# Two products of 512 and 256 columns in place of three of 256: the feed-forward of a four-layer transformer stack

## The reference

```python
# first kind, D_FF = 2816, conv over 3 tokens
def conv_glu_ffn(h, w_gate, w_up, conv_w, w_down):
    gate = causal_dwconv(h @ w_gate, conv_w)
    return (jax.nn.gelu(gate, approximate=True) * (h @ w_up)) @ w_down
# second kind, D_FF_2 = 4096, and a gate over all of x behind it
    m = jnp.square(jax.nn.relu(h @ w_up)) @ w_down
    x = x + rmsnorm(m, g_post_mlp)
    x = x + jax.nn.sigmoid(x @ w_ple_gate) * (p_i @ w_ple_proj)
```

## Time and profile before

| | |
|---|---|
| median of 3 runs | 1665.17 us (1662.94 to 1671.31) |
| the profiled execution | 1663.27 us |
| its span, first to last instruction | 1661.5 us |
| PE / DVE / ACT busy | 95% / 66% / 47% |
| mean granted TensorE clock | 0.974 of 2.4 GHz |

### The profile page before, as it was taken

One profiled execution on the slowest core, in us unless ns is written; L12 is line 12 of the kernel. 1 busy time (PEld: TensorE's weight loads), 2 busy tenths in 40 slices (PEclk: granted clock), 3 DMA queues, 4 the chain that ended last, 5 costly groups with the idle time before them and its releaser, 6 DMA issues.

```text
span 1661.5 us, 29327 instructions
## 1 busy us (share of the span) xinstructions
PE 1570.3 (95%) x11996; PEld 1402.5 (84%) x11996; DVE 1096.8 (66%) x1593; ACT 777.1 (47%) x1167; POOL 0.2 (0%) x4
## 2 busy tenths in 40 slices
PE   7998988999999989799999899899999989899998
PEld 7986568998898856799989788799889888799887
DVE  3765667776477576677754887666455698766545
ACT  4534254444445333644444365755345346755434
POOL 0000000000000000000000000000000000000000
PEclk9999898999999979899999899999999989999999
DMA  7521033655642201465554333455555333355553
GB/s 252 164 71 52 1 98 122 203 179 200 193 142 68 78 27 35 135 199 180 201 192 126 101 107 120 137 188 196 193 187 141 121 102 102 127 178 192 201 178 102
DMA packets 186310, 232.23 MB, mean 140 GB/s; under 512 B 22560, under 2 KB 161600, under 8 KB 186048
## 3 DMA queue, kind: packets, MB, share of 16 engines
q1 hardware_dynamic: 186176, 230.34, 43.0%
HBM read 229.28 MB, written 1.05 MB: 139 GB/s over the span
## 4 chain that ended last, share of the span: by engine, by line
PE 81%; DVE 7%; ACT 4%; DVEq 2%; issue 2%; DMA 2%; ACTq 1%; SPq 0%
PE banks L434 80%; DVE all_ring_rounded L2759 1%; ACT all_ring_rounded L2577 1%; DVE all_rest L2928 1%; DVE all_work L2863 1%; DMA all_ring<-in_w_in 1%; DMA all_ring<-in_w_ple_gate 1%; DVEq L2862 1%; PE banks L2242 1%; DVE all_work L2825 1%; PE banks L928 0%; DVE all_work L2821 0%; DVE all_work L2847 0%; ACT all_work L345 0%; DVEq L2823 0%
## 5 line engine op out<-in xcount | busy, mean ns | idle before, releaser
L434 PE MATMUL banks<-all_mix_rounded,all_ring_rounded 128*128 128x256 f32 (+2 forms) x3584 | 661.0, 285 | 15.6 <-DVEq L430 12.1
L434 PEld LDWEIGHTS banks<-all_mix_rounded,all_ring_rounded 128*128 128x128 f32 (+2 forms) x3584 | 561.6, 191 | 24.5 <-DVEq L430 13.7
L434 PE MATMUL banks<-all_work_rounded,all_ring_rounded 128*128 128x256 f32 x1792 | 508.1, 284 | 0.0
L434 PE MATMUL banks<-all_ring_rounded,all_work_rounded 128*128 128x512 f32 (+1 forms) x1856 | 463.0, 377 | 0.7 <-DVE all_ring_rounded L2759 0.7
L434 PEld LDWEIGHTS banks<-all_ring_rounded,all_work_rounded 128*128 128x128 f32 x1856 | 349.1, 189 | 66.3 <-issue 2.3
L434 PEld LDWEIGHTS banks<-all_work_rounded,all_ring_rounded 128*128 128x128 f32 x1792 | 343.2, 192 | 1.3 <-issue 1.0
L2759 DVE TENSOR_TENSOR all_ring_rounded<-all_ring,all_ring_rounded 128x2048 fp32r<-128x2048 f32 x104 | 237.6, 2291 | 137.5 <-ACT all_ring_rounded L2577 134.5
L1610 DVE TENSOR_TENSOR all_ring_rounded<-all_ring,all_ring_rounded 128x2048 fp32r<-128x2048 f32 (+2 forms) x96 | 214.1, 2233 | 87.5 <-ACT all_ring_rounded L1367 84.6
L2577 ACT ACTIVATE all_ring_rounded<-all_ring 128x2048 fp32r<-128x2048 f32 x104 | 198.2, 1910 | 152.5 <-DMA all_ring<-in_w_mlp_down 87.4
L1367 ACT ACTIVATE all_ring_rounded<-all_ring 128x2048 fp32r<-128x2048 f32 (+2 forms) x96 | 177.9, 1860 | 93.0 <-DMA all_ring<-in_ffn_w_down 42.3
L434 PE MATMUL banks<-all_work 64*64 64x64 f32 (+10 forms) x2084 | 169.5, 275 | 22.5 <-ACT all_work L2581 5.5
(11 more groups left out here) (263 smaller groups left out, 1232.7 us busy)
## 6 DMA issues: line engine op xcount, KB each, us to landing
all_ring<-in_w_in SPq DMA_DIRECT2D x48, 1024.0 KB, 5.4
all_ring<-in_w_mlp_up SPq DMA_DIRECT2D x32, 1024.0 KB, 5.4
all_ring<-in_w_mlp_down SPq DMA_DIRECT2D x32, 1024.0 KB, 4.9
all_ring<-in_ffn_w_gate SPq DMA_DIRECT2D x22, 1024.0 KB, 5.4
all_ring<-in_ffn_w_up SPq DMA_DIRECT2D x22, 1024.0 KB, 5.5
all_ring<-in_ffn_w_down SPq DMA_DIRECT2D x22, 1024.0 KB, 5.0
all_ring<-in_w_out SPq DMA_DIRECT2D x16, 512.0 KB, 4.2
all_ring<-in_w_out SPq DMA_DIRECT2D x8, 1024.0 KB, 5.0
```

What stands on the lines that cost most here:

```text
L434: ins = self.nc.tensor.matmul(out, lhsT, rhs, start=start, stop=stop)
```

## The change

In gate, up and block 2's up, a k tile takes two products. The weights' high part now streams against both parts of h at once, 512 columns, into a whole bank: high by high in its first half, high by low in its second. The weights' low part streams against h's high part, 256 columns, into the first half. What the PE no longer adds up is added by others: ACT copies the second half out, and DVE adds the first half to the copy. For this, gate and up get a bank each. In block 1, the convolution's first step (a product with one weight per partition) goes from DVE to ACT, the rounding of the product too, and the low part is taken one step later. ACT rounds the next panel in the middle of its step. In block 2 the relu is merged into DVE's square. `w_ple_gate`'s panels are cut in four k tiles by 512 columns. The two areas of h's parts become one tensor.

```diff
+    def mm_wide(self, out, w, k):
+
+        h = self.hi_and_lo[:, :, k, :]
+        if k < KT - 1:
+            self.mm(shaped(out, 2, T), w[0], h, k == 0, False)
+        last = self.mm(out[:, 0:T], w[1], h[:, 0, :], False, False)
+        if k == KT - 1:
+            last = self.mm(shaped(out, 2, T), w[0], h, False, True)
+        return last
...
@@ rows_by
-            for k in range(KT):
-                last = self.mm3(banks[q // 2][:, (q % 2) * 256:(q % 2) * 256 + 256], [a[:, k, t * P:(t + 1) * P] for a in lhs],
-                                [a[:, k, :] for a in w], k == 0, k == KT - 1)
+            for k in range(4):
+                at = 4 * (q % 2) + k
+                last = self.mm3(banks[q // 2], [a[:, at, t * P:(t + 1) * P] for a in lhs], [a[:, k, :] for a in w], at == 0, at == KT - 1)
...
@@ block 1, PE
-            c, b = (j % 2) * P, psum.bank(f"ff{j}")
+            c, name = (j % 2) * P, f"{('gate', 'up')[half]}_{j}"
+            b = psum.claim(pe, name)
             for k in range(KT):
-                last = mm3(b[:, half * T:(half + 1) * T], [a[:, k, c:c + P] for a in w], [a[:, k, :] for a in h], k == 0, k == KT - 1)
+                last = kit.mm_wide(b, [a[:, k, c:c + P] for a in w], k)
+            last.then_inc(psum.full_of(name), 1)
...
@@ block 1, ACT
-        for j in range(FT):
-            q = j // 2 + 1
-            name = f"{('gate', 'up')[j % 2]}{q}" if q < FT // 2 else f"down{j - FT + 2}"
-            round_weights(name)
-            act.wait_ge(*psum.filled(f"ff{j}"))
-            if j >= 2:
-                act.wait_ge(*due("ff_conv", j - 1))
-            A_(gpad[:, j % 2, 2:2 + T], psum.bank(f"ff{j}")[:, 0:T], ACT.Copy).then_inc(S["ff_gate"], 1)
-            act.wait_ge(*due("ff_conv", j + 1))
-            A_(gcv[:, j % 2, 2, :], gcv[:, j % 2, 1, :], ACT.Gelu_apprx_tanh).then_inc(S["ff_gelu"], 1)
+        for j in range(FT + 1):
+            if j < FT:
+                if not j:
+                    round_weights(panel_at(0))
+                act.wait_ge(*psum.filled(f"gate_{j}"))
+                A_(gpad[:, j % 2, 2:2 + T], psum.bank(f"gate_{j}")[:, T:2 * T], ACT.Copy).then_inc(S["ff_gate"], 1)
+                act.wait_ge(*psum.filled(f"up_{j}"))
+                A_(gl[:, j, :], psum.bank(f"up_{j}")[:, T:2 * T], ACT.Copy).then_inc(S["ff_up"], 1)
+                act.wait_ge(*due("ff_added", j + 1))
+                A_(gcv[:, j % 2, 0, :], gpad[:, j % 2, 2:2 + T], ACT.Copy, scale=fw[:, j, 2:3]).then_inc(S["ff_scaled"], 1)
+                if j < FT - 1:
+                    round_weights(panel_at(j + 1))
+            if j:
+                act.wait_ge(*due("ff_prod", j))
+                A_(rounded(gh[:, j - 1, :]), gcv[:, (j - 1) % 2, 2, :], ACT.Copy).then_inc(S["g_hi"], 1)
+            if j < FT:
+                act.wait_ge(*due("ff_conv", j + 1))
+                A_(gcv[:, j % 2, 2, :], gcv[:, j % 2, 1, :], ACT.Gelu_apprx_tanh).then_inc(S["ff_gelu"], 1)
...
@@ block 1, DVE (its former loop and finish(j) go)
+        def add_first_half(out, name):
+            return V.tensor_tensor(out, psum.bank(name)[:, 0:T], out, ALU.add)
+
+        def low_part(j):
+            dve.wait_ge(*due("g_hi", j + 1))
+            V.tensor_tensor(rounded(gl[:, j, :]), gcv[:, j % 2, 2, :], as_float32(rounded(gh[:, j, :])), ALU.subtract)
+            dve.drain().then_inc(S["gT"], 1)
...
+        for j in range(FT + 1):
+            if j < FT:
+                subtract_rounded(panel_at(j))
+                if j >= 2:
+                    low_part(j - 2)
+                dve.wait_ge(*due("ff_gate", j + 1))
+                add_first_half(gpad[:, j % 2, 2:2 + T], f"gate_{j}").then_inc(*psum.freed(f"gate_{j}"))
+                dve.drain().then_inc(S["ff_added"], 1)
+                dve.wait_ge(*due("ff_up", j + 1))
+                add_first_half(gl[:, j, :], f"up_{j}").then_inc(*psum.freed(f"up_{j}"))
             if j:
...
+                dve.wait_ge(*due("ff_gelu", j))
+                dve.drain()
+                V.tensor_tensor(gcv[:, (j - 1) % 2, 2, :], gcv[:, (j - 1) % 2, 2, :], gl[:, j - 1, :], ALU.mult).then_inc(S["ff_prod"], 1)
+            if j < FT:
+                dve.wait_ge(*due("ff_scaled", j + 1))
...
@@ block 2, panels
-    late += [(f"2{layer}.ple{i}", wgate[layer, :, :, 256 * i:256 * i + 256], KT, 0, 256) for i in range(4)]
+    late += [(f"2{layer}.ple{2 * half + n}", wgate[layer, :, 4 * n:4 * n + 4, 512 * half:512 * half + 512], 4, 0, 512)
+             for half in range(2) for n in range(2)]
...
@@ block 2, ACT
-                act.wait_ge(*psum.filled(f"ff{c}"))
-                A_(gh[:, 2 * c:2 * c + 2, :], shaped(psum.bank(f"ff{c}"), 2, T), ACT.Relu).then_inc(*psum.freed(f"ff{c}"))
-                act.drain().then_inc(S["ff_relu"], 1)
+                for half in range(2):
+                    act.wait_ge(*psum.filled(f"ff{c}{half}"))
+                    A_(gh[:, 2 * c + half, :], psum.bank(f"ff{c}{half}")[:, T:2 * T], ACT.Copy).then_inc(S["ff_half"], 1)
...
@@ block 2, DVE
-                V.tensor_tensor(gl[:, 2 * c:2 * c + 2, :], gh[:, 2 * c:2 * c + 2, :], gh[:, 2 * c:2 * c + 2, :],
-                                ALU.mult).then_inc(S["ff_squared"], 1)
+                for half in range(2):
+                    part = gh[:, 2 * c + half, :]
+                    dve.wait_ge(*due("ff_half", 2 * c + half + 1))
+                    V.tensor_tensor(part, psum.bank(f"ff{c}{half}")[:, 0:T], part, ALU.add).then_inc(*psum.freed(f"ff{c}{half}"))
+                dve.drain()
+                V.scalar_tensor_tensor(gl[:, 2 * c:2 * c + 2, :], gh[:, 2 * c:2 * c + 2, :], 0.0, gh[:, 2 * c:2 * c + 2, :],
+                                       ALU.max, ALU.mult).then_inc(S["ff_squared"], 1)
```

More of the change, by code:

```diff
@@ L313, in __init__ @@
         self.nc = nc
+        self.hi_and_lo = shaped(rounded(columns(0, 2 * KT * T)), 2, KT, T)
         self.x, self.columns, self.rounded, self.hT, self.mixT = x, columns, rounded, hT, mixT
@@ L640 @@
     1, "b_exp": 1, "erow": 1, "hid": 1, "decays": 1, "nt": 1, "act": 2, "lb_max": 1, "lb_exp": 1, "ff_conv": 22, "ff_gate": 22, "ff_gelu": 22,
-    "kr_done": 1, "dve": 70, "log_f": 2, "lf_tok": 2, "e_ready": 16, "kq": 16, "masked": 14, "last_scores": 2, "vf": 14, "weighed": 16, "level_U": 6,
+    "kr_done": 1, "dve": 48, "log_f": 2, "lf_tok": 2, "e_ready": 16, "kq": 16, "masked": 14, "last_scores": 2, "vf": 14, "weighed": 16, "level_U": 6,
+    "ff_scaled": 22, "ff_prod": 22, "g_hi": 22, "ff_up": 22, "ff_added": 22,
 }
@@ L760, in panels1, with panel_at @@
     return panels[:FIRST + 1] + with_parts(panels[FIRST + 1:] + late)
+def panel_at(j):
+    q = j // 2 + 1
+    return f"{('gate', 'up')[j % 2]}{q}" if q < FT // 2 else f"down{j - FT + 2}"
 def block1(nc, ctx, kit, banks, ring_all, A):
@@ L1344, in tensor @@
         for j in range(FT):
-            psum.claim(pe, f"ff{j}")
             for half in range(2):
-                last = gate_up(j, half)
-            last.then_inc(psum.full_of(f"ff{j}"), 1)
+                gate_up(j, half)
         def wait_product(n):
@@ L2011, in vector @@
         dve.drain()
-        for j in range(FT):
-            q = j // 2 + 1
-            name = f"{('gate', 'up')[j % 2]}{q}" if q < FT // 2 else f"down{j - FT + 2}"
-            subtract_rounded(name)
-            dve.wait_ge(*due("ff_gate", j + 1))
-            step(V.tensor_scalar(gcv[:, j % 2, 0, :], gpad[:, j % 2, 2:2 + T], fw[:, j, 2:3], None, ALU.mult))
-            step(V.scalar_tensor_tensor(gcv[:, j % 2, 1, :], gpad[:, j % 2, 1:1 + T], fw[:, j, 1:2], gcv[:, j % 2, 0, :], ALU.mult, ALU.add))
-            V.scalar_tensor_tensor(gcv[:, j % 2, 1, :], gpad[:, j % 2, 0:T], fw[:, j, 0:1], gcv[:, j % 2, 1, :], ALU.mult, ALU.add).then_inc(S["ff_conv"], 1)
-            if j:
-                finish(j - 1)
-        finish(FT - 1)
+        for j in range(FT + 1):
[8 more added lines that the diff above has]
+                add_first_half(gl[:, j, :], f"up_{j}").then_inc(*psum.freed(f"up_{j}"))
+            if j:
+                dve.wait_ge(*due("ff_gelu", j))
[3 more added lines that the diff above has]
+                dve.wait_ge(*due("ff_scaled", j + 1))
+                step(V.scalar_tensor_tensor(gcv[:, j % 2, 1, :], gpad[:, j % 2, 1:1 + T], fw[:, j, 1:2], gcv[:, j % 2, 0, :], ALU.mult, ALU.add))
+                V.scalar_tensor_tensor(gcv[:, j % 2, 1, :], gpad[:, j % 2, 0:T], fw[:, j, 0:1], gcv[:, j % 2, 1, :], ALU.mult, ALU.add).then_inc(S["ff_conv"], 1)
+        low_part(FT - 2)
+        low_part(FT - 1)
         for i in range(2, FT // 2):
@@ L2528, in up @@
             w = kit.split_panel(pe, ring, f"up{c}")
-            b = psum.bank(f"ff{c}")
+            b = psum.claim(pe, f"ff{c}{half}")
             for k in range(KT):
-                last = mm3(b[:, half * T:(half + 1) * T], [a[:, k, half * P:(half + 1) * P] for a in w], [a[:, k, :] for a in h], k == 0, k == KT - 1)
-            return last
```

(10 more changed lines are left out.)

11 lines of the change are left out of this document (3 added, 8 removed).

## The result

| | before | after |
|---|---|---|
| median | 1666.12 us, 4 runs (1662.94 to 1671.31) | 1652.51 us, 4 runs (1651.24 to 1653.44) |
| ratio of the two | | 0.9917, 95% interval 0.9903 to 0.9932 |
| profiled execution / its span | 1663.27 / 1661.5 us | 1653.44 / 1651.6 us |

The kernel became 13.6 us faster by the medians. The forecast was a gain of 19.5 us and 1645 us, with a range of 1640 to 1656. So the direction and the range were right, and 70% of the forecast gain came.

The account below looks back on a forecast made before the run. TensorE, busy 95% of the span, was taken as the bound, with an extra 13.3 ns per product. Terms 9.2 + 6.8 + 2.6 - 1.0 + 1.9 = 19.5 us gave a forecast of 1645 us, range 1640 to 1656.

Parts of the forecast that it names:

- Fewer products: Gate, up and block 2's up: each k tile drops one product's extra 13.3 ns, saving 9.2 us and 6.8 us.
- The extra stays with the run: Rival: each 256-column run keeps its extra, a 512 product takes 240 ns, k tile stays 360; 1660 us, chance 0.08.
- a slow loop: Rival: DVE and ACT's loop paces block 1's gate stage; 1653 us at 5.82 us per tile; chance 0.12 for 5.75 to 6.1.
- The waits of the gate stage: Block 1's gate stage: ten PE waits of 0.26 us go if the new loop is quick enough, 2.6 us gained.
- The new loop's waits: Block 1's gate stage: DVE and ACT loop of 5.62 us against PE's 5.55 per tile costs 0.5 us per layer, -1.0 us.
- Block 2's up stage: The extra copy and additions on ACT and DVE fit in their idle time; nothing on the path.
- Gate panels: Block 2's gate panels: 12 products of 512 replace 24 of 256, 0.16 us each for six per layer, 1.9 us gained.
- the first two panels gain nothing: Block 2's gate panels, each layer: what the first two save turns into PE wait for the third panel's subtraction.

Follow-up runs that it names:

- only512: Changed kernel with all products of the weights' low part left out in gate, up and block 2's up, only wide ones remaining; 1595.41 us.
- grouped: Changed kernel with each half tile's products reordered: seven of 512 columns, the eight of 256, then the last of 512; 1652.27 us, ratio to before 0.991.
- contig: Changed kernel whose wide product streams two neighbouring k tiles of h's high part, one run of 512 columns, giving another result; one run of 1655.34 us.
- beside: Changed kernel with h's two parts stored side by side for each k tile, same result; 1652.72 us, ratio to before 0.9909.
- three: Changed kernel with three products of 256 columns per k tile in place of the two, all else as changed; 1657.89 us, ratio to before 0.9946.
- link: Changed kernel with block 1's scaled copy issued twice on ScalarE, a drain between; 1673.28 us, ratio to before 1.0035.
- ple_only: Kernel before with only block 2's gate panels cut in four k tiles by 512 columns; 1666.04 us, ratio 0.9993.

## Why the prediction was right, and where its size was off

*Fewer products, 9.2 + 6.8 us.* The mechanism was right, and the saving stands in the stages that it names; the term was mis-sized: 7.5 ns per k tile and not 13.3, so 5.3 and 3.8 us, 9.1 in place of 16. The step that failed is "one extra of 13.3 ns goes": it priced a pair of 512 and 256 as the sum of a long run of each. `only512` shows that the 226.7 ns is right for the run, `grouped` that the excess stands where the length changes. The rows of before show no such alternation, and the prediction bounded the operand's two places but not the mixture of lengths. A bound for it, from nothing saved to all of the 13.3 ns, would have said that the term was 0 to 16 us.

*The extra stays with the run.* As told, this rival fell: `contig` and `beside` exclude the two places as a reason, and `only512` shows the wide product at 226.7 ns and not at 240. Something else gave back nearly half of the term, so the result lies just half way between the forecast of 1645 and this rival's 1660. That it still lay in the stated range is owed to the range's width, which was drawn for a slow loop and not for this.

The Trainium skill ("TensorE: Matmul & The Clock Gate", "Back-to-back issue gap") would have this part worth 3 us by an estimate from its 2.5 ns per product. Measured are 9.1, between that and the prediction; the runs of one length agree with 13.3 ns, not with 2.5.

*The waits of the gate stage, 2.6 us.* `three` gave 2.7 with no wait left. Right.

*The new loop's waits, -1.0 us.* L was forecast at 5.62 and is 5.60, idle time 0.43 for "about 0.5"; the cost is one stall of 1.0 in layer 1 and none in layer 0. Right in sum. It came in the way foretold (a gate panel lands late, one loop behind it is too long), but by a landing of 7.3 us and not by twenty small lags: with a pair at 352.5 PE needs 5.64 us, more than the loop. The mis-sized term thus hid part of the other risk, which was luck, though not much of it: in `grouped` PE needs 2 x 2.793 = 5.59 us per tile, and there layer 1 has one wait of 1.2 us, layer 0 none, and the down stages are 0.4 us longer each. `link` confirms the price and shows that the risk was real.

*Block 2's up stage, nothing on the path.* Right: 256 pairs, no wait, and 256 times the pair's price is the stage.

*Gate panels, 1.9 us.* By the stages 0.9 and 1.0; by the whole not to be told from nothing. The wait ahead of the third panel was forecast to grow from 1.58 to 1.9 us, and it is 1.31:

```profile
1241.41 4.83 PE L435 MATMUL banks<-all_ring_rounded,all_work_rounded 128*128 128x512 f32 x20 [1.31 <-DVE all_ring_rounded L2795]
```

The subtraction that PE waits for came earlier too, counted from the start of the down stage. The statement that the first two panels gain nothing was therefore wrong for the whole change: PE reaches the third panel 0.5 us sooner in each layer, 1.0 us that the sum lacks (0.3 and 0.5 between the second executions of both). In `ple_only` the wait did grow, so this gain needs the rest of the change. `three` has it as well (96.74 and 96.66 us), so it isn't the wide products that bring it; what does is open.

*The sum.* 5.3 - 0.1 + 3.8 + 2.7 - 1.0 + 1.9 = 12.6 us, and 13.6 with the 1.0 ahead of the third panel. The table's stages give 12.8 and with the same 1.0 us 13.8; the medians 13.6 (11.3 to 16.2 by the interval). That these agree so closely is partly chance: the profiled spans differ by only 9.9, for what the stages outside the change lost.

## What to carry to other kernels

When products of two lengths are to alternate, don't price them by runs of each: nearly half of the gain can stay in the changes of length, and only a run that mixes them, or a bound that allows for it, tells. When work moves from the bound engine to two helpers, write their loop down link by link from rows and compare it with the new pace of the bound engine; the sum was right to 0.02 us here, and one link more would have made the change a loss. Before shortening such a loop by reordering a queue, ask what each moved instruction then waits for: both orders tried here put something late (a load, a rounding) in front of something ready.

## What the runs showed of the hardware

The price of a float32r product depends on its neighbours: 512 columns take 226.7 ns in a run of their own (`only512`) and 235.4 between two of 256 (after), which in turn take 117.0 and not 120. Behind eight of 256 the first five of 512 take 228 to 236, and only from the sixth on is it 227 (`grouped`). Why stays open.

Some stretches of about 3 us at the 1.2 GHz level come at places that change from one execution to the next. Windows at the start of layer 1's projection, which the change doesn't touch, in the kernel after and in the second execution of before:

```profile
470.00:473.00 3.00, 3.00 (x17) 3.00 (x16) 2.68 (x8) 0.00 (x0) 0.00 (x0) 0.52 0.79 214
```

```profile
473.00:476.00 3.00, 3.00 (x16) 3.00 (x15) 2.68 (x8) 0.00 (x0) 0.00 (x0) 0.50 0.78 227
```

The clock is 0.52 and 0.50. In the first execution of before that stage began at 1.00 and took 34.65 us to its first plain product in place of 36.14. PE had been idle for 1.48 us ahead of the stage in all three, so this idle time alone doesn't decide. Of the fourteen profiles, eight show this stretch at this place and six don't, and the kernel before is on both sides. It costs 1.5 us. Two or three such stretches are as much as the gains of `grouped` or `three`: a single profiled span doesn't tell a gain of that size, stage lengths do. `grouped` shows it: its gate stages are 0.9 and 0.6 us shorter, its up stages 0.55 and 0.7 us longer for their slow starts, its down stages 0.4 each, and as a whole it isn't quicker by anything these runs can tell.
